# Seven block products for eight in the gate and up projections of a feed-forward layer

## The reference, cut to what matters

```python
D_FF = 2816
def channel_and_ple(x, p, w13, w2, w_ple, w_gate, g, b):
    gate, up = jnp.split(x @ w13, 2, axis=-1)
    ffn = (jax.nn.silu(gate) * up) @ w2
    ple = jax.nn.sigmoid(x @ w_gate) * (p @ w_ple)
    return layer_norm(ALPHA * x + ffn + ple, g, b)
```

## Time and profile before

| | us |
|---|---|
| median of 3 runs | 3149.61 |
| lowest, highest run | 3135.89, 3150.36 |
| profiled execution, span | 3131.9 |

### The profile page before, as it was taken

One profiled execution on the slowest core, in us unless ns is written; L12 is line 12 of the kernel. 1 busy time (PEld: TensorE's weight loads), 2 busy tenths in 40 slices (PEclk: granted clock), 3 DMA queues, 4 the chain that ended last, 5 costly groups with the idle time before them and its releaser, 6 DMA issues.

```text
span 3131.9 us, 48828 instructions
## 1 busy us (share of the span) xinstructions
PE 3044.1 (97%) x19497; PEld 2865.8 (92%) x19497; DVE 1519.0 (49%) x2889; ACT 859.4 (27%) x1875; POOL 954.9 (30%) x471
## 2 busy tenths in 40 slices
PE   8998999999999999999989999989999999999997
PEld 8697778879999999999989999978899999999997
DVE  2897865444434333333564555565444333343336
ACT  2675454341110011111124544554301111100101
POOL 3132100045533343333222222212545333333430
PEclk9998999999999999999999999999999999999999
DMA  3130000012311111111022111111222111111101
GB/s 102 31 71 29 1 1 8 34 51 86 95 47 47 40 47 47 47 47 40 14 71 59 44 43 51 38 55 61 73 85 62 52 42 45 47 47 40 47 7 56
DMA packets 209372, 149.73 MB, mean 48 GB/s; under 512 B 28914, under 2 KB 195764, under 8 KB 209236
## 3 DMA queue, kind: packets, MB, share of 16 engines
q1 hardware_dynamic: 209236, 147.85, 15.8%
HBM read 128.09 MB, written 19.73 MB: 47 GB/s over the span
## 4 chain that ended last, share of the span: by engine, by line
PE 89%; DVE 6%; issue 2%; ACT 1%; DMA 0%; PEld 0%; PEldq 0%; SPq 0%; POOL 0%; ACTq 0%; DVEq 0%; POOLq 0%
PE psum L153 50%; PE psum L2265 16%; PE psum L1823 6%; PE psum L713 4%; PE psum L684 2%; PE psum L1363 2%; PE psum L1395 2%; DVE junk L946 2%; PE psum L695 2%; PE psum L1379 1%; PE psum L647 1%; DVE bias L905 1%; PE psum L1338 1%; PE psum L1796 0%; PE psum L629 0%
## 5 line engine op out<-in xcount | busy, mean ns | idle before, releaser
L153 PE MATMUL psum<-x_hi,w_hi 128*128 128x352 f32 x3192 | 1036.9, 325 | 10.0 <-POOL x_lo L1785 4.1
L153 PE MATMUL psum<-x_hi,w_lo 128*128 128x352 f32 x3192 | 1024.0, 321 | 0.0
L153 PE MATMUL psum<-x_lo,w_hi 128*128 128x352 f32 x3192 | 1023.7, 321 | 0.0
L122 POOL TENSOR_TENSOR w_hi<-w_raw,zeros 128x1024 fp32r<-128x1024 f32 (+1 forms) x209 | 380.9, 1822 | 1543.2 <-PE psum L153 983.5
L153 PEld LDWEIGHTS psum<-x_hi,w_hi 128*128 128x128 f32 x3192 | 598.1, 187 | 12.2 <-issue 11.3
L153 PEld LDWEIGHTS psum<-x_lo,w_hi 128*128 128x128 f32 x3192 | 599.3, 188 | 0.5
L153 PEld LDWEIGHTS psum<-x_hi,w_lo 128*128 128x128 f32 x3192 | 597.8, 187 | 0.5
L124 POOL TENSOR_TENSOR w_lo<-w_raw,w_hi 128x1024 fp32r<-128x1024 f32 (+1 forms) x209 | 485.4, 2323 | 16.4
L2518 DVE TENSOR_TENSOR gate<-psum,gate 128x352 f32<-128x352 f32 x120 | 63.0, 525 | 725.3 <-PE psum L153 725.3
L2265 PE MATMUL psum<-h_hi,w_hi 128*128 128x352 f32 x1056 | 341.0, 323 | 2.1 <-DVE h_lo L2540 1.6
L2483 DVE TENSOR_TENSOR o_col<-psum,o_col 128x352 f32<-128x352 f32 x528 | 263.1, 520 | 156.4 <-PE psum L2265 154.3
(11 more groups left out here) (562 smaller groups left out, 3997.0 us busy)
## 6 DMA issues: line engine op xcount, KB each, us to landing
w_raw<-in_ffn_w_dram SPq DMA_DIRECT2D x132, 512.0 KB
w_raw<-in_b_w_in_dram SPq DMA_DIRECT2D x24, 512.0 KB
w_raw<-in_ple_w_gate_dram SPq DMA_DIRECT2D x16, 512.0 KB
x_nat<-in_x_prompt_dram SPq DMA_DIRECT2D x8, 512.0 KB, 7.8
w_raw<-in_a_w_in_dram SPq DMA_DIRECT2D x8, 512.0 KB
w_raw<-in_a_w_in_dram SPq DMA_DIRECT2D x16, 256.0 KB
x_rows<-x_rows SPq DMA_DIRECT2D x8, 512.0 KB, 2.6
out_new_b_v_prompt_dram<-valsB SPq DMA_DIRECT2D x8, 512.0 KB, 3.4
```

What stands on the lines that cost most here:

```text
L122: nc.gpsimd.tensor_tensor(c.w_hi[s][:, 0:kc], c.w_raw[s][:, 0:kc], zero, ALU.add).then_inc(c.split[s], 1)
L153: last = c.nc.tensor.matmul(out, w, x, start=(n == 0), stop=(n == 3 * len(terms) - 1))
```

## The change

For pairs 1 to 9 of both layers, gate and up are each computed by Strassen's method in Winograd's form. The weights of a gate (or up) pair are a 2x2 block matrix: A11, A12 are unit j=0 with the lower and upper half of the width, A21, A22 are unit j=1. The inputs x are 2x2 as well: two halves of the width by token pieces 0 and 1. Seven block products take the place of eight; piece 2 is computed plainly with the same four A blocks. The four weight sums S1 to S4 are made by GpSimd, five adds of 128x512 for a gate or up pair, in the buffer of the low part; GpSimd also makes both parts of every block, as before, but of half size. The input sums T1, T2, T4 are made once a layer by VectorE and ScalarE, at the start of pair 0; T3 takes the place of x in piece 1 of the lower half between pair 0 and pair 10 (`difference`). VectorE puts the results together from PSUM with 14 more adds a pair (`quarter`), four of the six gate-by-up products then read SBUF on both sides, and ScalarE keeps one product a gate or up pair (`keep_first`).

The ring becomes four slots in eight half blocks of 128x512, plus slots 4 and 5 for D0 and D1 of the last pair. The feed-forward part has two raw buffers; a unit n waits for the last read of unit n - 2. The loops are written out. The loads of the norm's gain and shift move to just ahead of the last pair's D0.

```diff
-SLOTS = 6
+SLOTS = 4
+HALVES = 2 * SLOTS
...
+    PARTS = ("A11", "S2", "S1", "A12", "S3", "A22", "S4", "A21")
+    PLACES = ((0, 2), (0, 0), (1, 1), (1, 0), (0, 1), (1, 2))
...
+    def first_block(i):
+        return 0 if i == 0 else 12 + 20 * (i - 1)
+    def part_block(i, pair, k):
+        return first_block(i) + 8 * pair + k
+    def down_block(i, j):
+        return first_block(i) + (8 if i in (0, L) else 16) + 2 * j
...
+    def raw_free(eng, i, u):
+        if u in (D0, D1):
+            eng.wait_ge(s_wl, b_wu + down_block(i, u - D0) + 2)
+        elif i in (0, L):
+            eng.wait_ge(s_wl, b_wu + plain_block(i, u) + 2)
+        elif u in (G0, U0):
+            eng.wait_ge(s_wl, b_wu + part_block(i, int(u == U0), 3) + 1)
+            eng.wait_ge(s_sum, b_sum + 10 * (i - 1) + 5 * int(u == U0) + 5)
+        else:
+            eng.wait_ge(s_wl, b_wu + part_block(i, int(u == U1), 7) + 1)
+    def block_free(eng, n):
+        if n >= 200:
+            eng.wait_ge(s_wu, b_wu + first_block(L))
+        elif n >= HALVES:
+            eng.wait_ge(s_wu, b_wu + n - HALVES + 1)
...
+    def ffn_unit(sp, i, u):
+        n = ORDER[i, u]
+        r = n % 2
+        if n >= 2:
+            raw_free(sp, *next(x for x, m in ORDER.items() if m == n - 2))
...
+        sp.dma_start(dst, src).then_inc(s_ld[r], 16)
...
-        with g.Fori(0, L) as i:
-            for u in range(6):
-                split_unit(c, g, fn, i, u, KC)
+        def low(n, src):
+            hi, lo = block(n)
+            block_free(g, n)
+            nc.gpsimd.tensor_tensor(hi, src, zero, ALU.add).then_inc(s_wh, 1)
+            g.wait_ge(s_wh, b_wu + n + 1)
+            nc.gpsimd.tensor_tensor(lo, src, hi.bitcast(F32), ALU.subtract).then_inc(s_wl, 1)
...
+        def pair_low(i, pair):
...
+            raw_ready(g, i, u0)
+            raw_ready(g, i, u1)
+            block_free(g, at["S1"])
+            nc.gpsimd.tensor_tensor(s1, a21, a22, ALU.add).then_inc(s_sum, 1)
+            g.wait_ge(s_sum, sums + 1)
+            nc.gpsimd.tensor_tensor(s2, s1, a11, ALU.subtract).then_inc(s_sum, 1)
+            g.wait_ge(s_sum, sums + 2)
+            low(at["A11"], a11)
+            low(at["S2"], s2)
+            low(at["S1"], s1)
+            low(at["A12"], a12)
+            block_free(g, at["S4"])
+            nc.gpsimd.tensor_tensor(s3, a11, a21, ALU.subtract).then_inc(s_sum, 1)
+            nc.gpsimd.tensor_tensor(s4, a12, a22, ALU.subtract).then_inc(s_sum, 1)
+            g.wait_ge(s_sum, sums + 4)
+            nc.gpsimd.tensor_tensor(s4, s4, s3, ALU.add).then_inc(s_sum, 1)
+            low(at["S3"], s3)
+            low(at["A22"], a22)
+            g.wait_ge(s_sum, sums + 5)
+            low(at["S4"], s4)
+            low(at["A21"], a21)
...
+        for i in range(1, L):
+            pair_low(i, 0)
+            pair_low(i, 1)
+            for j in (0, 1):
+                unit_low(i, D0 + j, down_block(i, j))
```

```diff
-                if at_end:
-                    mm.then_inc(c.used[s], 1)
+            if at_end:
+                mm.then_inc(s_wu, 4)
...
+        def down_ready(i):
+            pe.wait_ge(s_wl, b_wu + down_block(i, 1) + 2)
...
+        def pair_products(i, pair):
+            a, d, b, cc, e = (at((6 + x) % 8, TP) for x in ((0, 1, 2, 3, 4), (5, 6, 7, 0, 1))[pair])
...
+            pe.wait_ge(s_wl, b_wu + n + 1)
+            pe.wait_ge(s_da, adds + (20, 23)[pair])
+            part_product(n, a, x_part(0, 0), True, True)
+            part_product(n, d, x_part(0, 2), True, False).then_inc(s_wu, 1)
...
+            part_product(n + 1, b, t2, True, True).then_inc(s_wu, 1)
...
+            part_product(n + 2, cc, t1, True, True).then_inc(s_wu, 1)
...
+            part_product(n + 3, a, x_part(1, 0), True, True)
+            part_product(n + 3, d, x_part(1, 2), False, True).then_inc(s_wu, 1)
...
+            part_product(n + 4, b, x_part(0, 1), True, True).then_inc(s_wu, 1)
...
+            part_product(n + 5, e, x_part(1, 2), True, False)
+            pe.wait_ge(s_v, sums + 3)
+            part_product(n + 5, b, t4, True, True).then_inc(s_wu, 1)
...
+            part_product(n + 6, cc, x_part(1, 1), True, True).then_inc(s_wu, 1)
...
+            part_product(n + 7, e, x_part(0, 2), False, True).then_inc(s_wu, 1)
```

VectorE's side, the order of an up pair:

```diff
+        def up_pair(i):
...
+            done(4)
+            quarter(i, first[:, :], 5, first[:, :], 0)
+            gated(i, 0, at((6 + 6) % 8, TP))
+            v.wait_ge(s_v, sums + 9)
+            gated(i, 1, first[:, :])
+            done(5)
+            quarter(i, third[:, :], 7, second[:, :], 8)
+            quarter(i, second[:, :], 0, second[:, :], 8)
+            quarter(i, first[:, :], 0, third[:, :], 10)
+            low_h(i, 0)
+            v.wait_ge(s_v, sums + 12)
+            gated(i, 2, first[:, :])
+            low_h(i, 1)
+            done(6)
+            quarter(i, third[:, :], 7, third[:, :], 10)
+            low_h(i, 2)
+            v.wait_ge(s_v, sums + 13)
+            gated(i, 3, third[:, :])
+            done(7)
+            quarter(i, second[:, :], 0, second[:, :], 11)
+            low_h(i, 3)
+            v.wait_ge(s_v, sums + 14)
+            gated(i, 4, second[:, :])
+            done(8)
+            gated(i, 5, at((6 + 1) % 8, TP))
+            low_h(i, 4)
+            low_h(i, 5)
...
+        x_sum(t1_tmp, x12l, x11l, ALU.subtract, 0)
+        x_sum(t1_sum, x12h, x11h, ALU.subtract, 0)
+        x_sum(t1_sum, t1_sum, t1_tmp, ALU.add, 2)
+        x_sum(t2_sum, x22h, t1_sum, ALU.subtract, 3)
+        x_sum(t2_sum, t2_sum, x22l, ALU.add, 4)
+        x_sum(t4_sum, x21h, t2_sum, ALU.subtract, 5)
+        x_sum(t4_sum, t4_sum, x21l, ALU.add, 6)
```

More of the change, by code:

```diff
@@ new lines, in unit_low @@
+        def unit_low(i, u, n):
+            raw_ready(g, i, u)
+            for half in (0, 1):
+                low(n + half, raw_half(raw_of(i, u), half))
+        def pair_low(i, pair):
+            u0, u1 = ((G0, G1), (U0, U1))[pair]
+            r0, r1 = raw_of(i, u0), raw_of(i, u1)
+            a11, a12, a21, a22 = raw_half(r0, 0), raw_half(r0, 1), raw_half(r1, 0), raw_half(r1, 1)
+            at = {part: part_block(i, pair, k) for k, part in enumerate(PARTS)}
+            s1, s2, s3, s4 = (block_sum(at[x]) for x in ("S1", "S2", "S3", "S4"))
+            sums = b_sum + 10 * (i - 1) + 5 * pair
+            raw_ready(g, i, u0)
[19 more added lines that the diff above has]
+            low(at["A21"], a21)
@@ L2269, in down, with plain_product @@
-            if not at_end:
+            if at_end:
+                mm.then_inc(s_wu, 4)
+            else:
                 mm.then_inc(s_d, 1)
+        def down_ready(i):
+            pe.wait_ge(s_wl, b_wu + down_block(i, 1) + 2)
+        def plain_product(i, u, t, o, sem):
+            n = plain_block(i, u)
+            pe.wait_ge(s_wl, b_wu + n + 2)
+            terms = []
+            for half in (0, 1):
+                (hi, lo), (xh, xl) = block(n + half), x_part(half, t)
+                terms += [((hi[:, k, :], lo[:, k, :]), (xh[:, k, :], xl[:, k, :])) for k in range(KC // 2)]
+            mm = product(c, o, terms)
+            if t < PIECES - 1:
+                mm.then_inc(sem, 1)
+            else:
+                mm.then_inc(s_wu, 2)
@@ L2285, in tensor @@
         pe.wait_ge(s_sg, b_sg + 3 * KC)
[L2286 to L2305, removed]
-            for t in range(PIECES):
[L2307 to L2317, removed]
@@ L2319, in gate_last @@
+        for i in range(1, L):
+            pair_products(i, 0)
+            pair_products(i, 1)
+            downs(i)
         def gate_last(j, t):
-            s = unit_ready(c, pe, fn, L, 2 * j)
+            if j == 0 and t == 1:
+                pe.wait_ge(s_tv, b_tv + 18)
             if j == 1:
@@ L2509, in vector, with x_read @@
         v.wait_ge(s_acc, b_acc + 3 * KC)
[L2510 to L2523, removed]
-            for t in range(PIECES):
-                for m in range(KC):
-                    add_down(i, t, m, at((6 + m) % 8, TP))
+        def x_read(k, t):
+            hi, lo = x_part(k, t)
+            return hi.bitcast(F32), lo.bitcast(F32)
@@ new lines, in x_sum, with low_sum, difference @@
+        def x_sum(out, a, b, op, done):
+            if done:
+                v.wait_ge(s_tv, b_tv + done)
+            nc.vector.tensor_tensor(out, a, b, op).then_inc(s_tv, 1)
+        def low_sum(hi, lo, total, done):
+            v.wait_ge(s_th, b_th + done)
+            nc.vector.tensor_tensor(lo, total, hi.bitcast(F32), ALU.subtract).then_inc(s_tv, 1)
+        def difference(done):
+            (ah, al), (bh, bl), (dh, dl) = x_read(1, 1), x_read(0, 1), x_plain(0, 1)
+            x_sum(dh, ah, bh, ALU.subtract, 0)
+            x_sum(dl, al, bl, ALU.subtract, 0)
+            x_sum(dl, dl, dh, ALU.add, done + 2)
@@ new lines, in downs_added, with quarter, gated @@
+        def downs_added(i, pos):
+            for n in pos:
+                t, m = divmod(n, KC)
+                add_down(i, t, m, at((6 + DOWN[n]) % 8, TP))
```

(26 more changed lines are left out.)

315 lines of the change are left out of this document (272 added, 43 removed).

## The result

| | before | after |
|---|---|---|
| median of 4 runs | 3149.99 | 3364.93 |
| lowest, highest | 3135.89, 3152.62 | 3355.32, 3372.57 |
| profiled execution, span | 3131.9 | 3369.3 |

The changed kernel takes 1.0692 of the time before, 95% interval 1.0653 to 1.0731: 215 us slower. 3349 was forecast, with a range of 3250 to 3415.

What follows compares the result with a forecast made beforehand. The bound was to move from PE to GpSimd's chain: 79.5 us a pair for 68.7, +194 over 18 pairs, plus 5 for edges, gives 3331 on the span, 3349 us carried over to the median; range 3250 to 3415.

Steps and rivals of the forecast that it cites:

- The bound moves to GpSimd's 40 instructions: Changed pairs, downs' end to next downs: GpSimd needs 51.9 us, PE's products 42.0, so GpSimd sets the period.
- The price of half-size instructions: GpSimd's 128x512 hi and lo: 2.36 us together, on a line between 1024 and 256 columns; ends 2.16 and 2.76.
- The U1 load: Before the up pair's first sum: the whole raw-buffer load stands in GpSimd's path, 3.8 us a pair.
- Contention: GpSimd beside two-input VectorE instructions in a changed pair: ten meetings of 0.2 us, 2.0 us; ends 0 and 3.0.
- second rival: GpSimd loses a whole VectorE instruction, 0.52 us, at each of ten meetings a pair: +58, 3407 us; chance 0.12.
- The clock: Start of each downs: after PE's 7 us standstill, half rate for 4.8 us loses 2.4 us; ends 0 and 2.9.
- The sum of a pair: One changed feed-forward pair: 51.9 + 2.0 + 0.3 + 2.4 + 22.9 = 79.5 us, 10.8 over 68.7; 18 pairs +194.
- The edges: Layer starts and pairs 0, 9 and 10: some 2.5 us a layer in pair 0, 5 in all (0 to 10).
- The carried-over 17.7 us: Profiled span lay 17.7 us under the runs' median; this was added to the forecast span of 3331, giving 3349.
- PE as the bound: Rival for changed pairs: GpSimd fits within PE's 42.0 us, so the kernel gets faster, 3081 us; chance 0.04.
- a clock low through the up part: Rival: PE's clock stays at 0.5 through the up part, +12 us more a pair, 3565 us; chance 0.05.
- The lock in full: Rival on the shared port: GpSimd loses 5.2 us a pair for 2.0, +58 in all, 3407 us; chance 0.12.

Runs made afterwards that it cites:

- kept-warm run: Changed kernel with 44 extra unused matmuls per changed pair where TensorE waits for the last down block: 3331.28 us, 1.0615 of before.
- the base once more: The changed kernel, unedited, measured again on the chip of the next three experiments as their base: 3359.92 us, 1.0705 of before.

## Why the prediction was right

The cause, the place and the sign were right; the size was 199 for 215, and for 220.6 if the mixer's 16.8 us are left out of the two profiled spans. By its own steps:

- **The bound moves to GpSimd's 40 instructions.** Shown by the stretch of 54.5 us with PE's wait at its end, by the missing sums (12.5 us a pair back) and by the hi parts on ScalarE (15.1 us a pair back, to PE's own 64.9).
- **The price of half-size instructions** by the line: 1.04 and 1.29 measured, the same line gives 1.04 and 1.28. The step with the widest bounds was exact. Neither end (2.16 or 2.76 a pair of instructions) was near the 2.36 measured (1082.56 to 1084.92).
- **The U1 load** 3.8 us: it was 3.85 to 4.14, and worth 4.0 when left out. The D1 load was hidden, as forecast.
- **Contention** 2.0 us a pair, measured 2.2. The number held, the reading behind it only for 352 columns. The prediction took 0.16 to 0.30 us as what GpSimd pays for any two-input VectorE instruction, and set this against a lock. The Trainium skill ("SBUF — State Buffer", Who interferes with whom) calls the shared port pair an exclusive lock. The traces agree with it up to the 0.2 to 0.4 us above, on both sides: h_lo 0.52 alone and 1.36 beside GpSimd, GpSimd's hi 1.04 alone and 2.42 beside 1408 columns. The lock's price for h_lo was just 0.13 to 0.28 us, and not the 0.52 of the second rival.
- **The clock** 2.4 us, worth 2.0 to 2.3 by the kept-warm run. The gap is 8.2 us, not "nearly 7": six of the ten stretched instructions lie behind A21's lo, and make the down lows 1.3 us later.
- **The sum of a pair**: 80.0 us on average for 79.5 (they alternate between some 79.5 and 80.7, with the clock low for 6.8 or 10.2 us), 18 pairs +204 for +194. The load and the contention were each 0.2 larger.
- **The edges** were the mis-sized term: 5 us forecast, 17 measured (220.6 - 204). In pair 0 the forecast had 2.5 us a layer; it was 5.7 and 5.3. I had priced the three instructions of 128x1408 at 1.7 us with short waits. They took 2.3 to 2.7 us beside GpSimd, so PE waited 3.74 us for its bank, and this brought the clock down to half for 3.4 us, which had no term of its own at the edges. In pair 9 the forecast said "it lies in PE's wait", at nothing. It cost some 2 us in each (82.3 and 82.0 us): VectorE's part does lie in PE's wait, but it stretched GpSimd's last hi and lo before the downs by 2.6 us, and these are in the path. The rest, about 1 us, is at the ends of the layers.

The carried-over 17.7 us between span and median is no property of a span. The mixer, with the same code, took 16.8 us longer in the profile after than in the one before. Like for like, the forecast was 21.6 us short (199 for 220.6), and that it is 16 us by the medians is chance.

The rivals: PE as the bound (3081 us) is what happened only with 20 hi parts gone from GpSimd; a clock low through the up part didn't occur: in the profile after, each fall in pairs 1 to 9 began in the gap (the base once more had three falls of 3.4 us outside it, at 1017, 2656 and 2898 us). The lock in full, at 0.52 us a meeting (3407 us), didn't occur: 2.2 us a pair and not 5.2.

## What to carry to other kernels

Busy shares over the span don't say whether work can be added to an engine: lay its instructions between the two events that the ring of buffers ties together, here "last down" to "next down", and compare that stretch with the bounding engine's. A method that saves products on one engine has to be paid on engines that have slack within that stretch; here the same 7-for-8 was 7% slower with both weight parts on GpSimd and 2% faster with the high parts on ScalarE. And when a tile is halved, price it by the line through two measured sizes, and count the loads that lost their spare buffer. What GpSimd loses to a VectorE instruction with two SBUF inputs is to be priced by the length of that instruction.

## What the runs showed of the hardware

- 44 useless matmuls a pair, in a waiting time, made the kernel about 29 us faster (9 to 47): a gap of 8.2 us had left TensorE at 1.2 GHz for 3.1 us of the next products in the pair shown (until 1052.1) and for 5.5 us in the one after it (until 1134.0).
- The high part of 128x512 float32 in fp32r takes 0.61 us as a copy on ScalarE and 1.04 on GpSimd (adding zeros).
- Where GpSimd met a VectorE instruction with two SBUF inputs, each lost the length of the other's less 0.2 to 0.4 us. GpSimd lost 0.13 to 0.28 us to one of 0.52, 0.93 to one of 1.21, and 1.23 or 1.38 to one of 1.61. So the length of the other engine's instruction matters, and not only the number of meetings.
- The same unchanged code, layer 0's mixer, ended 16.8 us later in one execution than in another. In 300 to 600 us the mean granted clock was 0.91 in the one and 0.96 in the other.
